# Expert rows of a PEER layer: 32 of 512 gathered rows moved from the preparing steps into the 128 slots

## The chip, the cores and the metric

One core of one Trainium2 chip runs the whole program. The metric is device time in microseconds (us), lower is better, as the median of several runs. TensorE is the matmul engine, VectorE, ScalarE and GpSimd the three others that compute, SyncE issues transfers; the profile calls them PE (PEld for weight loads), DVE, ACT, POOL and SP. Sixteen DMA engines serve the core.

## The reference

Two blocks of a transformer run one behind the other on 512 tokens of width 1024. The change lies in the last large part of the second, the PEER layer: product-key retrieval of experts that are single neurons. For each token, eight heads pick 16 of 16,384 experts each, so 128 experts a token, with softmax weights `g`:

```python
ue = jnp.take(u, ids, axis=0)          # (tokens, heads, 16, 1024)
ve = jnp.take(v, ids, axis=0)
a = jax.nn.gelu(jnp.einsum('cd,chkd->chk', xc, ue), approximate=False)
return jnp.einsum('chk,chkd->cd', (g * a).astype(xc.dtype), ve)
```

## The kernel before, in words

`peer_experts` (L2222) splits the 512 tokens in two halves of 256.

**Sparse half (tokens 0 to 255): gathered rows.** For a tile of 128 tokens (one on each partition) and one of the 128 picks, a *row* is an indirect transfer of 128 x 1024 float32 (512 KB): for each token the table row of its own expert. `row(n)` (L2256) numbers the 512 rows: 128 of `u` and then 128 of `v` for tile 0, and the same for tile 1. A u row is used by one multiply-and-sum on VectorE, the dot product with the token (L2520). After 128 of them ScalarE takes their Gelu (L2447, in `gelu_dots`, which waits until VectorE has used the last one), VectorE multiplies by the softmax weights (L2513), and the 128 v rows are scaled by these and added up (L2524 for the first two, L2527). Rows land in a ring of 8 buffers (`RING`), which lie in the space of xT and hT; GpSimd fetches them (`fetch_rows`, L2332) six rows ahead of their use.

**Dense half (tokens 256 to 511): all experts.** The 128 *slots* (the loop `for s in range(NKEY)` of each engine) stand for 128 experts each. In a slot TensorE multiplies the slot's tile of u (split into a high and a low part by ScalarE L2418 and VectorE L2542, three products each, L110 to L112) with the 256 tokens; ScalarE takes the Gelu (L2463); VectorE multiplies by the slot's gates, which is the slot product L2568; TensorE multiplies with the slot's tile of v into `y_ps` (`down`, L2392). SyncE loads two tiles of 512 KB a slot (`peer_ut` L2297 and `peer_v` L2305), three of each held.

**Gates.** A token's gate for an expert is the softmax weight if it is picked, else 0. They are made in 128 groups of 8 tokens and a quarter of the slots (32) each: one-hots of one half of the expert's number (`one_hot`: on ScalarE as eight squares L2426 and one Relu L2429; in the first 32 groups the even ones on VectorE, L2482), a comparison for the other half (`one_hot_first`, VectorE L2494, one buffer), its product with the weights (`weighed`, GpSimd L2323), eight matmuls on TensorE (`gates`, L2372), and taking the result from PSUM (`take`: ScalarE L2437, VectorE L2504). One-hots, products and PSUM results have two buffers, by the group's parity.

**Order of the work.** Each engine's instructions are issued in one fixed order. The first quarter's 32 groups are made in 32 *preparing steps*, numbered -32 to -1, before slot 0; slot s makes group s + 32 on the side, until slot 95. In the steps before groups 8 and 16 the first two u tiles are split too. `dealt(step)` (L2242) says how many rows VectorE has used by the end of a step or slot: `EARLY` (32) in the preparing steps, one each, and the other 480 over the 128 slots, 3.75 each (three, four, four, four). `use_rows` (VectorE, last thing in each step and slot), `fetch_rows` (GpSimd, `asked` = `dealt` + 6) and `gelu_dots` (ScalarE) all go by it.

```python
    def dealt(step):
        if step < 0:
            return max(0, EARLY * (step + GROUPS + 1) // GROUPS)
        return EARLY + (ROWS - EARLY) * (step + 1) // NKEY
```

By this count tile 0's last u row is used in slot 25 and tile 1's in slot 93, the v rows from slots 26 to 59 and 94 to 127.

Of the kernel before, what the change touches and what calls it, by code (L numbers as in the profile page):

```python
# [2221 lines left out]
def peer_experts(nc, C, xT, hT, h_tok, stream, ids, weights, ut, u, v, u_in, y, x_d):  # L2222
# [10 lines left out]
    GROUPS = DENSE // GROUP  # L2233
    assert GROUPS == QUARTER
    QUARTERS = NKEY // QUARTER
    ROWS = 2 * GT * PICKS
    EARLY = GROUPS
    tok0 = GT * P
    h_dense = hT[:, :, tok0:S]
    rows = [(xT, hT)[r // 4][:, r % 4 * 2:r % 4 * 2 + 2, :].rearrange("p k s -> p (k s)") for r in range(RING)]  # L2240
# [1 line left out]
# [6 lines that stand above are left out]
# [481 lines left out]
def block2(nc, A, C, xT, hT, mod):  # L2729
# [4 lines left out]
    with ExitStack() as ctx:  # L2734
# [48 lines left out]
        with ExitStack() as c2:  # L2783
# [18 lines left out]
            def to_tokens(dve, i, tile):  # L2802
                t, cols, k, toks = at(i)
                return nc.vector.tensor_copy(h_tok[:, t, cols], tile)
            turn(nc, C, GT * KT, lambda i: hT[:, at(i)[2], at(i)[3]], to_tokens)
            peer_experts(nc, C, xT, hT, h_tok, stream, ids, weights, A["peer_ut"], A["peer_u"], A["peer_v"], u_in, yt,
                         dram("x_kept", (P, KT * S)))

# [130 lines left out]
```

## Time and profile before

| | us |
|---|---|
| median of 3 runs | 3567.9 (3562.22 to 3570.99) |
| the profiled execution, its own time | 3575.29 |
| its span | 3573.4 |
| TensorE busy (share of the span) | 3068.4 (86%) |
| VectorE busy | 2337.9 (65%) |
| ScalarE busy | 1389.5 (39%) |
| GpSimd busy | 1101.5 (31%) |
| slot product L2568, first and last start | 2543.8 and 3527.4 |
| DMA, mean over the span | 174 GB/s |

The shares are means over stages that differ; the experts' stage is the last third, from about 2408 us (first transfer of `peer_ut`) to about 3532. In rows of a timeline the first number is the start, the second the duration, and brackets at the end give how long the engine had been idle before and what it waited for. A row `x3` merges three instructions of the same kind. Busy time by stage has for each engine the busy us and the number of instructions, then the granted TensorE clock as a share of its full 2.4 GHz (0.50 is 1.2 GHz), the busy share of the DMA engines and the GB/s that they moved.

### The profile page before, as it was taken

What the parts mean: (1) busy time and instruction counts of PE and PEld (TensorE: products, weight loads), DVE (VectorE), ACT (ScalarE), POOL (GpSimd) and SP (SyncE); (2) the same over time, 40 slices, a digit from 0 to 9 for tenths busy, and PEclk for the clock granted to TensorE, in tenths of its full rate; (3) what the DMA queues carried; (4) which work ended last, traced back from release to release, by engine and by line L of the source; (5) the groups of instructions that cost most, each with busy time, mean ns of one, the idle gap of its engine ahead of it and who ended that gap; (6) DMA issues with size and microseconds to landing.
All of it is one profiled execution on the core that took longest, in us unless ns stands there. A gap on an engine that the chain in (4) does not pass through costs nothing. (4 is left out here: it accounts for less than half of the span.)

```text
span 3573.4 us, 42767 instructions
## 1 busy us (share of the span) xinstructions
PE 3068.4 (86%) x15044; PEld 2316.2 (65%) x15044; DVE 2337.9 (65%) x4087; ACT 1389.5 (39%) x2495; POOL 1101.5 (31%) x781
## 2 busy tenths in 40 slices
PE   7989899998989999995797895634799999999997
PEld 5846688786846678784586663534666776666664
DVE  4256455565347455474645435988998999998886
ACT  3254333212244433312324432115665666665211
POOL 0031000000021100000003101337888888888663
PEclk9969999998959999997898897865799999999998
DMA  5220233353330123351243111106699999999996
GB/s 195 86 80 1 71 94 94 135 182 141 101 91 1 60 88 96 118 194 66 71 137 80 38 48 53 54 20 201 237 377 367 397 406 390 374 377 371 409 409 257
DMA packets 206351, 622.14 MB, mean 174 GB/s; under 512 B 31440, under 2 KB 64624, under 8 KB 200272
## 3 DMA queue, kind: packets, MB, share of 16 engines
q1 hardware_dynamic: 132432, 351.21, 28.5%
q0 software_dynamic: 73728, 268.47, 19.8%
q8 instruction: 110, 1.80, 0.2%
q14 instruction: 81, 0.66, 0.1%
HBM read 598.75 MB, written 20.84 MB: 173 GB/s over the span
## 5 line engine op out<-in xcount | busy, mean ns | idle before, releaser
L110 PE MATMUL psum<-sbuf 128*128 128x512 f32 (+1 forms) x2720 | 1029.0, 378 | 171.1 <-POOL sbuf L2196 84.4
L111 PE MATMUL psum<-sbuf 128*128 128x512 f32 (+1 forms) x2720 | 962.0, 354 | 0.0
L112 PE MATMUL psum<-sbuf 128*128 128x512 f32 (+1 forms) x2720 | 961.2, 353 | 0.0
L110 PEld LDWEIGHTS psum<-sbuf 128*128 128x128 f32 x2720 | 522.8, 192 | 284.3 <-POOL sbuf L2196 86.3
L111 PEld LDWEIGHTS psum<-sbuf 128*128 128x128 f32 x2720 | 523.3, 192 | 106.1 <-issue 36.1
L112 PEld LDWEIGHTS psum<-sbuf 128*128 128x128 f32 x2720 | 521.6, 192 | 72.4
L2392 PE MATMUL psum<-sbuf 128*128 128x512 f32 x1024 | 492.0, 625 | 15.2 <-DVE sbuf L2568 15.2
L1379 POOL TENSOR_TENSOR sbuf<-sbuf 64x768 fp32r<-64x768 f32 (+2 forms) x22 | 29.2, 1328 | 1539.3 <-ACT sbuf L1325 1362.0
L2341 POOL DMA_INDIRECT sbuf<-peer_u,sbuf x256 | 397.4, 1552 | 64.4 <-issue 44.1
L2520 DVE CUSTOM_DVE_ANT_0 sbuf<-sbuf 128x1024 f32<-128x1024 f32 x256 | 379.5, 1510 | 39.7 <-DMA sbuf<-peer_u,sbuf 39.0
L2527 DVE SCALAR_TENSOR_TENSOR sbuf<-sbuf 128x1024 f32<-128x1024 f32 x252 | 339.6, 1385 | 30.9 <-DMA sbuf<-peer_v,sbuf 30.4
L2341 POOL DMA_INDIRECT sbuf<-peer_v,sbuf x256 | 313.6, 1225 | 115.2 <-DVE sbuf L2527 57.0
L2392 PEld LDWEIGHTS psum<-sbuf 128*128 128x128 f32 x1024 | 193.1, 199 | 216.3 <-issue 197.5
L2426 ACT ACTIVATE sbuf<-sbuf 128x128 fp32r<-128x128 f32 x896 | 272.8, 392 | 0.0
L2372 PE MATMUL psum<-sbuf 128*128 128x64 f32 x1024 | 158.8, 308 | 114.0 <-DVE sbuf L2482 52.2
L496 DVE TENSOR_TENSOR sbuf<-sbuf 128x1024 fp32r<-128x1024 f32 x88 | 107.6, 1225 | 207.4 <-ACT sbuf L492 206.9
L2372 PEld LDWEIGHTS psum<-sbuf 128*128 128x128 f32 x1024 | 152.7, 230 | 124.6 <-issue 58.2
L2463 ACT ACTIVATE sbuf<-psum 128x256 f32<-128x256 f32 x128 | 49.1, 384 | 408.3 <-PE psum L112 408.2
L1352 ACT ACTIVATE sbuf<-psum 128x512 f32<-128x512 f32 (+1 forms) x240 | 122.2, 510 | 196.5 <-PE psum L1103 105.3
L2323 POOL TENSOR_TENSOR sbuf<-sbuf 128x512 fp32r<-128x512 f32 x128 | 174.2, 1361 | 48.3 <-DVE sbuf L2494 47.0
L1137 PE MATMUL psum<-sbuf 128*65 128x512 f32 (+4 forms) x384 | 172.2, 537 | 12.0 <-ACT sbuf L1339 11.6
L492 ACT ACTIVATE sbuf<-sbuf 128x1024 fp32r<-128x1024 f32 x88 | 93.1, 1060 | 224.7 <-PE psum L112 224.7
(292 smaller groups left out, 4693.4 us busy)
## 6 DMA issues: line engine op xcount, KB each, us to landing
sbuf<-peer_ut SPq DMA_DIRECT2D x128, 512.0 KB, 8.2
sbuf<-peer_v SPq DMA_DIRECT2D x128, 512.0 KB, 6.7
sbuf<-w_ffn SPq DMA_DIRECT2D x88, 512.0 KB, 3.6
sbuf<-w_mod SPq DMA_DIRECT2D x24, 1024.0 KB, 5.1
sbuf<-w_down SPq DMA_DIRECT2D x16, 1408.0 KB, 6.3
sbuf<-w_fm SPq DMA_DIRECT2D x38, 512.0 KB, 4.6
sbuf<-w_out SPq DMA_DIRECT2D x24, 512.0 KB, 3.7
sbuf<-w_tm SPq DMA_DIRECT2D x10, 1024.0 KB, 5.5
```

The source lines that it names most:

```text
L110: nc.tensor.matmul(acc, w_high(k), x_high(k), start=(k == 0), stop=False)
L111: nc.tensor.matmul(acc, w_high(k), x_low(k), start=False, stop=False)
L112: mm = nc.tensor.matmul(acc, w_low(k), x_high(k), start=False, stop=(k == kt - 1))
L1137: mm = nc.tensor.matmul(summed[0:W, i % SUMS, x.q0[j]:S], v[0:x.kw[j], x.v, j, :], prob[0:x.kw[j], i % 2, j, x.q0[j]:S], start=(j == 0), s ...
L1352: nc.scalar.activation(prob[0:x.kw[j], i % 2, j, x.q0[j]:S], shifted[0:x.kw[j], (block0[i] + j) % 2, x.q0[j]:S], ACT.Exp, scale=HD ** -0.5 ...
L2323: nc.gpsimd.tensor_tensor(part[:, n % 2, :, :, :], equal[:, :, :].unsqueeze(2).to_broadcast([P, GROUP, 2, QUARTER]), halved[:, toks, :].bi ...
L2341: pool.indirect_dma_start(rows[n % RING], None, (u, v)[f], bass.IndirectOffsetOnAxis(ap=stream[:, t, j:j + 1], axis=0)).then_inc(gathered[ ...
L2372: mm = nc.tensor.matmul(g_ps[:, n % 2, 2 * j * QUARTER:2 * (j + 1) * QUARTER], hot[:, n % 2, j, :], part[:, n % 2, j, :, :], start=True, s ...
L2392: mm = nc.tensor.matmul(y_ps[:, 2 * t + half, :], w[:, s % 3, t * P:(t + 1) * P], v_in[:, s % HELD, half * S:(half + 1) * S], start=(s == ...
L2426: nc.scalar.activation(hot[:, n % 2, j, :], C.iota[:, :], ACT.Square, bias=picked[:, 1, at:at + 1], scale=-1.0).then_inc(squared, 1)
L2520: nc.vector.tensor_tensor_reduce(out=rows[r], in0=rows[r], in1=h_tok[:, t, :], scale=1.0, scalar=0.0, op0=ALU.mult, op1=ALU.add, accum_out ...
L2527: nc.vector.scalar_tensor_tensor(sums, rows[r], dots[:, t, j:j + 1], sums, ALU.mult, ALU.add).then_inc(used[r], 1)
```

## The change

`EARLY` goes from 32 to 0. `dealt` is then 0 for all preparing steps and 4 x (s + 1) for slot s, so each slot uses exactly four rows. `asked` is 6 in step -32 (seven before), stays 6 until slot 0, and goes on six ahead of use. The u rows of tile 0 are used in slots 0 to 31, its v rows in 32 to 63, tile 1's in 64 to 95 and 96 to 127. Nothing else changes; the same 512 rows are fetched and used in the same order.

```diff
@@ -2234,7 +2234,7 @@
     assert GROUPS == QUARTER
     QUARTERS = NKEY // QUARTER
     ROWS = 2 * GT * PICKS
-    EARLY = GROUPS
+    EARLY = 0
     tok0 = GT * P
     h_dense = hT[:, :, tok0:S]
     rows = [(xT, hT)[r // 4][:, r % 4 * 2:r % 4 * 2 + 2, :].rearrange("p k s -> p (k s)") for r in range(RING)]
```

## Rows read from the trace of the kernel before

**Rows 1.** The page's 40 slices of 89 us: GB/s moved by DMA.

```profile
GB/s 195 86 80 1 71 94 94 135 182 141 101 91 1 60 88 96 118 194 66 71 137 80 38 48 53 54 20 201 237 377 367 397 406 390 374 377 371 409 409 257
```

**Rows 2.** Busy time by stage: preparing steps, then the slots' four quarters.

```profile
core 0: us, PE busy (x) PEld busy (x) DVE busy (x) ACT busy (x) POOL busy (x), PEclk, DMA share, GB/s
2434.30:2538.10 103.80, 50.86 (x225) 49.01 (x226) 96.98 (x129) 61.34 (x156) 79.72 (x57) 0.50 0.54 162
2543.80:2803.70 259.90, 243.23 (x1276) 174.23 (x1276) 234.95 (x346) 166.39 (x392) 217.49 (x152) 0.95 0.96 361
2803.70:3044.70 241.00, 232.34 (x1278) 169.35 (x1277) 238.78 (x266) 162.93 (x382) 202.27 (x150) 1.00 1.01 398
3044.70:3305.70 261.00, 242.67 (x1274) 173.82 (x1273) 236.30 (x361) 159.97 (x376) 222.59 (x156) 0.96 0.98 375
3305.70:3531.80 226.10, 210.59 (x1007) 141.10 (x1005) 193.95 (x182) 40.24 (x62) 144.32 (x114) 0.98 1.03 409
```

**Rows 3.** Timeline, two preparing steps: start us, us, engine, line, operation.

```profile
2500.64 3.62 PE L2372 MATMUL psum<-sbuf 128*128 128x64 f32 x16 [3.15 <-DVE sbuf L2482]
...
2503.80 2.42 DVE L2520 CUSTOM_DVE_ANT_0 sbuf<-sbuf 128x1024 f32<-128x1024 f32 x1
2504.07 1.05 POOL L2323 TENSOR_TENSOR sbuf<-sbuf 128x512 fp32r<-128x512 f32 x1
2504.30 0.38 ACT L2437 ACTIVATE sbuf<-psum 128x256 f32<-128x256 f32 x1 [1.32 <-PE psum L2372]
...
2506.15 1.21 DVE L2482 TENSOR_TENSOR sbuf<-sbuf 128x1024 fp32r<-128x1024 f32 x1
2507.04 1.15 ACT L2429 ACTIVATE sbuf<-sbuf 128x1024 fp32r<-128x1024 f32 x1
...
2507.41 3.62 PE L2372 MATMUL psum<-sbuf 128*128 128x64 f32 x16 [3.15 <-DVE sbuf L2482]
```

**Rows 4.** Timeline, opening: first fetch, group 2's product, group 3's matmuls.

```profile
2418.79 1.11 POOL L2341 DMA_INDIRECT sbuf<-peer_u,sbuf  x1 [0.17 <-issue]
...
2428.82 1.06 POOL L2323 TENSOR_TENSOR sbuf<-sbuf 128x512 fp32r<-128x512 f32 x1
...
2432.36 1.89 PE L2372 MATMUL psum<-sbuf 128*128 128x64 f32 x8 [0.50 <-issue]
```

**Rows 5.** Timeline around the split of u before group 16.

```profile
2482.56 1.15 ACT L2429 ACTIVATE sbuf<-sbuf 128x1024 fp32r<-128x1024 f32 x1
...
2487.10 3.62 PE L2372 MATMUL psum<-sbuf 128*128 128x64 f32 x16 [7.32 <-DVE sbuf L2482]
```

**Rows 6.** VectorE's waits, last quarter: us in total, times, longest.

```profile
DVE sbuf L2527 <- DMA sbuf<-peer_v,sbuf: 30.4, 46, 1.3
```

**Rows 7.** VectorE's timeline: L2568 of slots 0, 25, 26, 32-34, 60, 93, 94.

```profile
2543.81 0.42 DVE L2568 TENSOR_TENSOR sbuf<-sbuf 128x256 f32<-128x256 f32 x1 [3.37 <-ACT sbuf L2463]
...
2744.76 0.41 DVE L2568 TENSOR_TENSOR sbuf<-sbuf 128x256 f32<-128x256 f32 x1
...
2755.08 0.43 DVE L2568 TENSOR_TENSOR sbuf<-sbuf 128x256 f32<-128x256 f32 x1 [2.38 <-ACT sbuf L2463]
...
2803.66 0.43 DVE L2568 TENSOR_TENSOR sbuf<-sbuf 128x256 f32<-128x256 f32 x1
...
2810.22 0.41 DVE L2568 TENSOR_TENSOR sbuf<-sbuf 128x256 f32<-128x256 f32 x1
...
2817.99 0.41 DVE L2568 TENSOR_TENSOR sbuf<-sbuf 128x256 f32<-128x256 f32 x1
...
3014.21 0.41 DVE L2568 TENSOR_TENSOR sbuf<-sbuf 128x256 f32<-128x256 f32 x1
...
3276.85 0.41 DVE L2568 TENSOR_TENSOR sbuf<-sbuf 128x256 f32<-128x256 f32 x1
...
3288.32 0.42 DVE L2568 TENSOR_TENSOR sbuf<-sbuf 128x256 f32<-128x256 f32 x1 [3.82 <-ACT sbuf L2463]
```

**Rows 8.** Timeline of ScalarE, the Gelu of the second 128 dots.

```profile
3284.19 0.31 ACT L2447 ACTIVATE sbuf<-sbuf 128x128 f32<-128x128 f32 x1 [8.21 <-DVE sbuf L2520]
```

## The prediction

> **What bounds the kernel now.** I read the page's slices first: the change touches only the experts' stage, the last third of the span, where DMA rises from some 200 GB/s to a plateau of 367 to 409 [rows 1]. Then busy time by stage [rows 2]. The 32 preparing steps (2434 to 2538 us) keep VectorE at 97 of 104 us while the transfers move 162 GB/s and TensorE is half idle. In the 128 slots everything is near full at once: DMA share 0.96 to 1.03, TensorE 93 to 96%, VectorE 86 to 99%. So the present kernel uses 32 rows in a stretch with idle DMA and puts 3.75 a slot, not 4, where DMA is full. The change gives that up.
>
> Last I read the order of time. A pair of steps [rows 3] takes 6.77 us (TensorE's 16 gate matmuls begin at 2500.64 and again at 2507.41), and VectorE is what it waits for: its one-hot of the even group (L2482) comes only at 2506.15, behind two row dots. A dot is drawn out to 2.4 us because it stands beside GpSimd's 1.05 us product (rows 3: 2503.80 and 2504.07).
>
> **The preparing steps without rows.** Without the dots, next in line is a loop between ScalarE and TensorE over the odd groups, whose one-hots share one buffer: ScalarE takes the gates at 2504.30, makes eight squares and ends its Relu at 2507.04 + 1.15 = 2508.19, so 3.89 us; then 8 gate matmuls, half of the 3.62 us, 1.81; two handoffs of about 0.07. That is 5.85 us a pair. VectorE's own remaining work (1.21 + 4 x 0.41) and GpSimd's two products (2 x 1.05) fit beside it. Between group 3 and group 31 are 14 pairs.
> - Now: from 2432.36 + 1.89 = 2434.25 [rows 4] to the end of the stretch [rows 2], 2538.1, so 103.9 us. 14 x 6.77 is 94.8; the other 9.1 are the two splits of u (before groups 8 and 16), where VectorE waits for ScalarE's split, splits, and only then makes the even one-hot: from the Relu's end (2482.56 + 1.15 = 2483.71) to the end of both groups (2487.10 + 3.62 = 2490.72) 7.0 us [rows 5].
> - After: 14 x 5.85 = 81.9, plus 2 x (7.1 - 1.9) = 10.4, since a normal pair then ends 1.9 after its Relu. Together 92.3: a gain of 11.6 us.
> - Opening: GpSimd's product for group 2 starts at 2428.82, behind seven row fetches begun at 2418.79 [rows 4]. Afterwards there are six, at about 1.25 apart, so it starts near 2426.3; with VectorE free, group 3 ends near 2431.1 and not 2434.25: 3.2 us.
> Sum: **-14.8 us**. Bounds: 0 (the steps bound elsewhere) and -19 (both splits hidden as well). ScalarE's way from group 31 to the first slot product stays the same length, and just moves forward. No instruction is dropped: the 32 row fetches and dots go to the slots.
>
> **The slots with four rows.** A slot loads 2 tiles of 512 KB and its rows of 512 KB (0.524 MB) each: 3.015 MB now, 3.146 after. At the 409 GB/s of the last quarter [rows 2] that is 7.37 and 7.69 us.
> - Last quarter: it is DMA's; VectorE there waited 30.4 us for v rows [rows 6]. 8 rows x 1.28 us = **+10.3**.
> - Second quarter (v rows, gates being made): VectorE is 99% busy and DMA at 398 GB/s. Slots of three and four rows take 6.56 and 7.77 (2803.66, 2810.22, 2817.99 in rows 7), and three of four slots have four. With four everywhere: 32 x 7.77 = 248.6 against 241: **+7.6**. TensorE, busy 232 / 32 = 7.3 us a slot there, stays just under.
> - First and third quarter (u rows): 25 slots in 200.95 us (2543.81 to 2744.76) and 33 in 262.6 (3014.21 to 3276.85), 8.04 and 7.96 a slot [rows 7], well above both the 7.37 of the bytes and the 7.47 that the second quarter's mix of slots needs ((3 x 7.77 + 6.56) / 4). Such a slot with four rows is not shown by itself. Lower bound 7.77 (as with v rows), upper 8.7 (the first quarter's 361 GB/s). I take 8.33: the 8.0 plus a quarter row at 1.21 (rows 7, 7.77 - 6.56) to 1.28 (DMA), which is also the same transfer rate held (3.015/8.0 = 377 GB/s; 3.146/377 = 8.34). 64 slots: 533.1.
> - The two handovers from u to v rows: ScalarE stops until the last dot (8.21 us [rows 8]), then makes a one-hot before its Gelu, and VectorE idles 3.82; a slot of 10.3 and one of 11.5 come of it [rows 7], each followed by a long one, about 5 to 6 us too much in all. The first moves from slot 25 to 31 and stays, 5.9. The second moves from slot 93 to 95, after which no one-hot is left: 1. So 533.1 + 6.9 = 540.0 for both quarters, against 259.9 + 261.0 = 520.9: **+19.1**.
>
> Slots: 10.3 + 7.6 + 19.1 = **+37.0 us**. All of it lies on the path, since no other work stands behind the slots: the stage ends with the last rows and the last slot.
>
> The DMA ceiling is the term to weigh. The rows show 409 GB/s at a share of 1.03. The Trainium skill (DMA: Bandwidth & Descriptors, Where 436 GB/s comes from) puts the ceiling of the 16 engines at 435 GB/s. By that a four-row slot would be 7.23 us and the last quarter 15 us shorter, the whole change about +7. The trace never shows such a rate, so I stay with 409.
>
> **Sum.** -14.8 + 37.0 = +22.2 us. The profiled execution took 3575.3 (span 3573.4), so it would take 3597.5; it lies 7.4 above the median of 3567.9, and the median would be 3567.9 + 22.2 = **3590 us**. A measurement of this kernel can tell about 0.3% (10.7 us) from no change.
>
> **Rivals.**
> - A, as forecast: 0.60. Its own range 3580 to 3601, u slots of 8.17 to 8.5.
> - B, faster: the even deal makes the u slots regular. They are jittery now (waits for rows, clock 0.95), and their rows come in 4, 4, 4, 3. If four-row u slots run like four-row v slots, 64 x (8.33 - 7.77) = 36 us go, so 22.2 - 35.8 = -13.6: 3554. It decides below 7.82 us a u slot ((22.2 + 10.7) / 64 is 0.51). For it: DMA moves only 361 and 375 GB/s there. Against: the share is 0.96 to 0.98 even so, which is 5% more engine time per byte than in the last quarter, and an even deal doesn't make a packet quicker. The Trainium skill (SBUF — State Buffer, SBUF: two separate sides) says that an engine's work cannot slow a transfer; by that the low rate would be thin demand and could rise to 409. The rows of the u quarters rather speak against it. 0.07.
> - C, no change: the jitter gives back part of that. Between 7.82 and 8.15 us a u slot the total is within 10.7 us; at the present 8.0 it is 22.2 - 64 x 0.33 = +1: 3569. 0.13.
> - D, slower still: TensorE's clock. In the second quarter TensorE is 96% busy and the granted clock 1.00; in the u quarters it is 93% busy and the clock 0.95 and 0.96 [rows 2]. Four rows leave it idle longer in every slot. If the second quarter falls to the level of the others, its slots go from 7.77 to 8.33: 32 x 0.56 = +18, 3608. 0.13.
> - E: the preparing steps gain nothing, because the chain from VectorE's comparison (L2494) over GpSimd's product (L2323) and back, one buffer long, is as slow as the dots were: 3605. Against it: 0.41 + 1.05 us and two handoffs are half of a step's 2.9. 0.07.
> - That the rows aren't moved can be excluded: the deal is 0 for every step below 0. Six rows are still fetched ahead, as now.
>
> **How the numbers follow.** Predicted time: A, 3590. The range 3570 to 3610 leaves out B and the lower half of C (0.07 + 0.07) and some 0.05 above D. Slower than 0.3%: A + D + E = 0.80; same 0.13; faster 0.07.
>
> **What the profile should show.** Pairs of steps of 5.8 to 5.9 us with TensorE's gates released by ScalarE's Relu (L2429), no longer by L2482; group 31 done near 2523, first L2568 near 2529; DMA nearly idle from 2435 to there. Slots of 7.77 in the second quarter without a short one; 7.69 in the last, at 409 GB/s; first to last L2568 near 1021 us (983.6 now, rows 7). Pairs still at 6.8, or u slots at 8.0 or less, would prove me wrong.

## The result and the profile after

The changed kernel takes **3609.0 us** (median of 4, 3601.74 to 3619.13) against 3569.07 (median of 4) for the kernel before in the same series: a ratio of 1.0116, interval 1.0094 to 1.0138. Slower by 40 us where 22 were forecast; the sign was right, the size nearly twice. The profiled execution took 3619.13 (span 3617.3, against 3573.4), 10 above its median.

The first view is the page of the changed kernel, GB/s by slice of 90 us, the counterpart of [rows 1]:

```profile
GB/s 191 88 77 1 71 93 94 143 169 143 99 87 1 68 90 99 131 183 44 90 156 38 37 71 41 41 82 24 328 373 373 379 403 396 366 376 362 409 409 254
```

The 201 and 237 GB/s at the end of the preparing steps have become 24 and the start of the plateau. The plateau still has its two levels: 362 to 376 in slices where u rows are dotted, 396 to 409 where v rows are added (379 is the slice behind 2803 us, with most of the first handover).

Busy time by stage of the changed kernel (us, then busy us of PE, PEld, DVE, ACT, POOL with instructions, granted clock, DMA share, GB/s), which answers to [rows 2]:

```profile
2434.00:2531.00 97.00, 56.54 (x242) 53.57 (x243) 42.94 (x76) 60.54 (x158) 31.89 (x31) 0.50 0.10 36
...
2536.45:2808.30 271.85, 243.00 (x1266) 173.15 (x1264) 246.09 (x385) 164.68 (x386) 236.21 (x160) 0.95 0.97 364
2808.30:3063.70 255.40, 245.59 (x1314) 176.68 (x1314) 250.11 (x259) 170.11 (x395) 207.61 (x161) 0.99 1.01 396
3063.70:3335.40 271.70, 246.54 (x1252) 174.01 (x1251) 243.95 (x383) 156.90 (x366) 234.67 (x158) 0.94 0.98 365
3335.40:3571.00 235.60, 207.86 (x998) 139.57 (x996) 199.09 (x186) 40.23 (x61) 157.86 (x124) 0.99 1.03 409
```

In the preparing steps VectorE is now busy 43 of 97 us and no longer the bound. Their pairs, in the timeline of the changed kernel (start, us, engine, line), as in [rows 3]:

```profile
2504.06 1.15 ACT L2429 ACTIVATE sbuf<-sbuf 128x1024 fp32r<-128x1024 f32 x1
...
2505.26 3.78 PE L2372 MATMUL psum<-sbuf 128*128 128x64 f32 x16 [2.12 <-ACT sbuf L2429]
...
2505.85 1.22 DVE L2482 TENSOR_TENSOR sbuf<-sbuf 128x1024 fp32r<-128x1024 f32 x1
...
2509.96 1.15 ACT L2429 ACTIVATE sbuf<-sbuf 128x1024 fp32r<-128x1024 f32 x1
...
2511.16 3.78 PE L2372 MATMUL psum<-sbuf 128*128 128x64 f32 x16 [2.12 <-ACT sbuf L2429]
```

From 2505.26 to 2511.16 is 5.90 us, released by ScalarE's Relu: 5.85 was forecast, with that releaser.

**Where the time went.** I divide the stage at fixed events: its first load of a u tile, and the first L2568 of slots 0, 32, 64, 96 and 127. All are us of one profiled execution; the rows below the second are the experiments.

| kernel | preparing | slots 0-31 (u) | 32-63 (v) | 64-95 (u) | 96-127 (v) | all slots |
|---|---|---|---|---|---|---|
| before | 135.5 | 259.8 | 241.0 | 261.0 | 221.7 | 983.5 |
| changed | 121.7 | 271.8 | 255.4 | 271.8 | 235.6 | 1034.6 |
| changed, again | 121.7 | 275.8 | 254.9 | 268.4 | 235.8 | 1034.9 |
| 16 rows early | 122.4 | 265.3 | 245.5 | 270.2 | 226.0 | 1007.0 |
| changed, no v tiles loaded | 121.7 | 278.6 | 253.9 | 275.8 | 199.9 | 1008.2 |
| before, no v tiles loaded | 134.5 | 249.8 | 242.2 | 263.7 | 195.3 | 951.1 |
| changed, product only | 121.1 | 253.2 | 254.9 | 248.2 | 234.2 | 990.5 |
| changed, light dot | 121.7 | 254.9 | 255.0 | 248.6 | 233.3 | 991.9 |
| changed, half product | 121.2 | 257.8 | 254.2 | 255.8 | 235.2 | 1003.0 |
| changed, late Gelu | 121.1 | 275.8 | 250.7 | 270.0 | 235.2 | 1031.7 |
| before, light dot | 135.6 | 248.7 | 240.5 | 245.1 | 222.1 | 956.5 |
| before, light dot, late Gelu | 134.6 | 240.7 | 239.4 | 237.7 | 225.2 | 943.0 |
| changed, v table | 121.7 | 273.7 | 255.5 | 269.6 | 234.6 | 1033.3 |

Of the 43.9 us between the two spans, 6.5 lie ahead of the stage, where the code is the same (its first u load is at 2408.3 before and 2414.8 after). The preparing steps give 13.8, the slots cost 51.1, and the rest is 0.1. So the stage itself loses 37.3.

**The queue that the forecast left out.** These are GpSimd's groups in the changed kernel, first in slots 0 to 31, then in 32 to 63 (line, form, count | busy us, mean ns | idle before them and what ended it). L2341 fetches a row, L2323 is the one-hot's product:

```profile
L2341 POOL DMA_INDIRECT sbuf<-peer_u,sbuf x122 | 191.1, 1566 | 32.5 <-issue 22.6 <-DVE sbuf L2494 8.5
L2323 POOL TENSOR_TENSOR sbuf<-sbuf 128x512 fp32r<-128x512 f32 x32 | 37.2, 1164 | 10.0 <-DVE sbuf L2494 9.4
...
L2341 POOL DMA_INDIRECT sbuf<-peer_v,sbuf x123 | 143.0, 1163 | 32.7 <-issue 30.1
L2323 POOL TENSOR_TENSOR sbuf<-sbuf 128x512 fp32r<-128x512 f32 x32 | 58.7, 1835 | 12.9 <-DVE sbuf L2494 12.9
```

And one u slot of GpSimd's timeline in the changed kernel:

```profile
2700.24 1.07 POOL L2323 TENSOR_TENSOR sbuf<-sbuf 128x512 fp32r<-128x512 f32 x1
2701.47 1.78 POOL L2341 DMA_INDIRECT sbuf<-peer_u,sbuf  x1 [0.16 <-issue]
2703.55 0.94 POOL L2341 DMA_INDIRECT sbuf<-peer_u,sbuf  x1 [0.30 <-issue]
2704.79 1.71 POOL L2341 DMA_INDIRECT sbuf<-peer_u,sbuf  x1 [0.30 <-DVE sbuf L2494]
2706.81 1.98 POOL L2341 DMA_INDIRECT sbuf<-peer_u,sbuf  x1 [0.31 <-issue]
2708.81 1.22 POOL L2323 TENSOR_TENSOR sbuf<-sbuf 128x512 fp32r<-128x512 f32 x1
```

The slot takes 8.57 us (2700.24 to 2708.81), and nothing in it is idle but 0.3 us ahead of each fetch, in which the engine issues. A fetch takes 0.94 us or nearly twice that. With the mean of the group a u slot costs GpSimd 4 x 1.56 + 3 x 0.30 + 0.16 + 1.16 = 8.46 us; slots 0 to 31 took 8.49 in the mean. In the slots with v rows the same engine, at the same four fetches, has a mean fetch of 1.16, waits 12.9 us ahead of its products for VectorE's comparison (L2494), and the median slot is 7.78. Busy shares hide this: 236.21 of 271.85 us is 87%, but with the issue gaps, 0.30 us ahead of 96 fetches and 0.16 ahead of 32, it is 270.1, or 99%. In the row above, 9.4 of the 10.0 us idle ahead of L2323 lie before the first product, where the window begins; between a fetch and the next product all gaps of the quarter together are 0.5 us. An engine that never waits for another's signal is not paced by TensorE, whose clock was 0.95 here, or by the transfers.

The kernel before had it all in its trace. GpSimd's groups in its slots 0 to 31:

```profile
L2341 POOL DMA_INDIRECT sbuf<-peer_u,sbuf x90 | 140.1, 1557 | 23.8 <-issue 15.6 <-DVE sbuf L2494 6.1
L2323 POOL TENSOR_TENSOR sbuf<-sbuf 128x512 fp32r<-128x512 f32 x32 | 41.5, 1298 | 13.6 <-DVE sbuf L2494 13.2
```

The fetch of a u row took 1.56 us there too. With 3.75 of them a slot, 2.75 x 0.30 + 0.16 of gaps and a product of 1.22 us (the mean of slots 0 to 24; the 1.30 of the row counts the longer ones of the last slots too), a slot is 5.84 + 0.98 + 1.22 = 8.04 us, and [rows 7] gave 8.04. That it agrees so well is in part chance: GpSimd waited another 6.8 us in these 25 slots, and 92 fetches fell into them, not 94. A quarter of a row more is 0.25 x 1.86, which makes 8.50: the slot that came. This sum I had not made.

### The profile page after: what moved, and what is told of

It is laid out like the page before. It is cut to its first block and busy times, and to the rows that moved or that the text cites. A ratio compares the mean times of both kernels' runs of the same rounds, so it can differ in the third digit from the quotient of the medians.

```text
span 3617.3 us, 42767 instructions
## 1 busy us (share of the span) xinstructions
PE 3096.0 (86%) x15044; PEld 2331.0 (64%) x15044; DVE 2315.5 (64%) x4087; ACT 1391.4 (38%) x2495; POOL 1094.7 (30%) x781
## 5 line engine op out<-in xcount | busy, mean ns | idle before, releaser
L2392 PE MATMUL psum<-sbuf 128*128 128x512 f32 x1024 | 501.9, 636 | 28.2 <-DVE sbuf L2568 28.2
L2341 POOL DMA_INDIRECT sbuf<-peer_u,sbuf x256 | 393.8, 1538 | 68.3 <-issue 48.1
L2520 DVE CUSTOM_DVE_ANT_0 sbuf<-sbuf 128x1024 f32<-128x1024 f32 x256 | 354.5, 1412 | 45.6 <-DMA sbuf<-peer_u,sbuf 44.0
L2527 DVE SCALAR_TENSOR_TENSOR sbuf<-sbuf 128x1024 f32<-128x1024 f32 x252 | 339.2, 1380 | 37.2 <-DMA sbuf<-peer_v,sbuf 37.0
L2341 POOL DMA_INDIRECT sbuf<-peer_v,sbuf x256 | 314.8, 1230 | 110.7 <-DVE sbuf L2527 55.0
L2323 POOL TENSOR_TENSOR sbuf<-sbuf 128x512 fp32r<-128x512 f32 x128 | 169.8, 1326 | 93.1 <-DVE sbuf L2494 92.1
```

What stands on the lines that cost most here:

```text
L2323: nc.gpsimd.tensor_tensor(part[:, n % 2, :, :, :], equal[:, :, :].unsqueeze(2).to_broadcast([P, GROUP, 2, QUARTER]), halved[:, toks, :].bi ...
L2341: pool.indirect_dma_start(rows[n % RING], None, (u, v)[f], bass.IndirectOffsetOnAxis(ap=stream[:, t, j:j + 1], axis=0)).then_inc(gathered[ ...
L2392: mm = nc.tensor.matmul(y_ps[:, 2 * t + half, :], w[:, s % 3, t * P:(t + 1) * P], v_in[:, s % HELD, half * S:(half + 1) * S], start=(s == ...
L2520: nc.vector.tensor_tensor_reduce(out=rows[r], in0=rows[r], in1=h_tok[:, t, :], scale=1.0, scalar=0.0, op0=ALU.mult, op1=ALU.add, accum_out ...
L2527: nc.vector.scalar_tensor_tensor(sums, rows[r], dots[:, t, j:j + 1], sums, ALU.mult, ALU.add).then_inc(used[r], 1)
```

## The experiments

The theories, by letter: **D**, the u slots go at the speed of the transfers, as my sum assumed. **V**, at the speed of VectorE's dots. **G**, at the speed of GpSimd's queue, whose fetches are drawn out beside the dots. **L**, a loop of ScalarE and TensorE sets the pair of preparing steps as soon as VectorE has no more than one row in it. The expectations of the runs without v tiles still use V for what is divided here into V and G.

**The changed kernel again**, unchanged, as the base of the first series.

> The changed kernel as it is, beside the others of this job. In its first profile the preparing steps gained 13.9 us and the 127 slot intervals cost 51.2 us, while 6.5 us of the 44 lay in stages before the experts. Theory S (slots cost more than forecast, the rest is scatter): median 37 to 41 us above the kernel before; in the profile again about 122 us from the first u tile's load to the first slot product, and about 1030 to 1035 us from the first to the last slot product. Rival N (most of the excess over the forecast of 22 us is scatter of one profile): median 20 to 30 us above, slot intervals near 1021 us.

3605.4 us (before 3570.24; ratio 1.0104, interval 1.0079 to 1.013), so 35.2 above, a little less than the 37 to 41 expected. The stage repeats within 0.3 us (121.7 and 1034.9), though single quarters differ by 4. So less than 4 us in one quarter proves nothing.

**Half of the rows early.**

```
-    EARLY = 0
+    EARLY = GROUPS // 2
```

> EARLY = 16: one row in every second preparing step, 496 over the slots (3.875 each). Theory L (a loop of ScalarE and TensorE bounds the pair of preparing steps at 5.9 us as soon as VectorE has no more than one row in it): pairs of 5.9 to 6.1 us, so the preparing steps keep nearly all of the 14 us gain, and the slots cost half of 51 us: +12 us on the kernel before, 3580. Rival P (rows cost the preparing steps in proportion): half of both, +19 us, 3588.

3584.57 us, ratio 1.0043 (1.0027 to 1.0059). The median is 14.3 above its kernel before, where 12 were expected. The preparing steps keep nearly all they gained (122.4, so 13.1 of 13.8), and the slots pay 23.5 of the 51.1. Sixteen of the 32 early rows, one in every second step, therefore cost 0.7 us where they stood; the other 16 cost 13.1 there.

**No v tiles loaded**, once on the changed kernel and once on the kernel before: the first tiles are used again and 2.6 MB instead of 3.1 MB are moved in a slot.

```
-                if s >= HELD:
-                    sp.wait_ge(y_made, s - HELD + 1)
-                sp.dma_start(v_in[:, s % HELD, :], v[s * P:(s + 1) * P, :]).then_inc(v_landed[s % HELD], 16)
+                if s < HELD:
+                    sp.dma_start(v_in[:, s % HELD, :], v[s * P:(s + 1) * P, :]).then_inc(v_landed[s % HELD], 16)
...
-                pe.wait_ge(v_landed[s % HELD], 16 * (s // HELD + 1))
+                pe.wait_ge(v_landed[s % HELD], 16)
```

> EARLY = 0, and the dense half's v tiles are loaded for the first three slots only and used again after that: 125 transfers of 512 KB less, the dense half's down products are made from the wrong tiles. A slot then moves 2.62 MB in place of 3.15, 6.4 us at 409 GB/s. Theory D (transfers bind the u slots and the last quarter): last quarter from 7.6 to about 6.5 us a slot (TensorE), u slots from 8.45 to 7.6 to 7.8, second quarter stays at 7.8 to 7.9 (VectorE); in all some 80 us less than the changed kernel, 3530. Rival V (VectorE and GpSimd get in each other's way over u rows, transfers are only slow because they are asked for late): u slots stay at 8.3 to 8.5, only the last quarter falls, 35 us less, 3574.

> The same with EARLY = 32: v tiles loaded for the first three slots only. Read against the EARLY = 0 kernel without v tiles. Theory D: the last quarter then costs the same with 3.75 and with 4 rows (TensorE's 6.5 us), u and v slots of the other quarters differ by VectorE's quarter row, 0.3 us each, 29 us in all, less the 14 us of the preparing steps: the EARLY = 0 kernel is 12 to 16 us slower. Rival V: the price of the rows is VectorE's and stays, EARLY = 0 is 30 to 40 us slower.

3577.72 us (ratio 1.002, 1.0006 to 1.0034) and 3541.53 us (0.993, 0.9906 to 0.9954): 36.2 us apart, as with all tiles loaded (35.2 in this series). Busy time by quarter and one wait of VectorE (total, times, longest) in the changed kernel without v tiles:

```profile
2530.70:2809.20 278.50, 245.87 (x1265) 175.15 (x1264) 236.05 (x384) 164.55 (x386) 242.70 (x160) 0.94 0.87 297
...
3063.20:3339.00 275.80, 247.06 (x1251) 173.49 (x1250) 233.38 (x384) 156.90 (x366) 240.62 (x157) 0.94 0.88 300
3339.00:3538.90 199.90, 199.01 (x999) 137.47 (x997) 195.84 (x187) 40.19 (x61) 149.52 (x125) 1.00 1.02 403
```

```profile
DVE sbuf L2519 <- DMA sbuf<-peer_u,sbuf: 36.2, 23, 3.7
```

The last quarter, which is DMA's, falls from 235.6 to 199.9. The u quarters do not fall at all, at 297 and 300 GB/s, and VectorE still waits for rows, up to 3.7 us at a time. With a sixth of the bytes gone and the rows still late, what they are late for is not the transfers: **D falls**. The row is asked for late. (In the kernel before, the first u quarter did get 10.0 us shorter without v tiles, and the third 2.7 longer; whether that is scatter is not shown.)

**The dot in another form of instruction.** First only the product, without the sum along the row:

```
-                    nc.vector.tensor_tensor_reduce(out=rows[r], in0=rows[r], in1=h_tok[:, t, :], scale=1.0,
-                                                   scalar=0.0, op0=ALU.mult, op1=ALU.add,
-                                                   accum_out=dots[:, t, j:j + 1]).then_inc(used[r], 1)
+                    nc.vector.scalar_tensor_tensor(rows[r], rows[r], C.ones[:, 0:1], h_tok[:, t, :],
+                                                   ALU.mult, ALU.mult).then_inc(used[r], 1)
```

> EARLY = 0, with the dot's multiply-and-sum (L2520) replaced by VectorE's three-operand product that v rows use (L2527), same tiles, no sum: the dots stay a constant, so the sparse half's sums are of wrong weights. Theory G (in u slots GpSimd sets the pace: four fetches of 1.56 us and gaps of 0.3 us, one product of 1.17, no idle time besides; the fetch is drawn out from 0.94 to 1.8 us by the form of VectorE's dot): fetches fall to the 1.16 us of v slots, u slots from 8.4 to 7.8 us, both u quarters together 35 to 45 us shorter: about 3565. Rival F (a fetch from the u table is slow by itself, or TensorE's clock makes the long slots): fetches stay at 1.5 us, u slots at 8.4 us, no change against the changed kernel, 3605.

3564.31 us, ratio 1.0002 (0.9988 to 1.0015): the whole loss against the kernel before with its old dot is gone with one line. Then the same instruction with the sum (`accum_out=dots[:, t, j:j + 1]`), so that the dot is complete:

> EARLY = 0, and the dot is made by the three-operand product with its sum written out (two instructions again, the second reads the accumulator); everything is computed. Theory G1 (the form of the multiply makes the fetches slow): u slots near 7.8 us, 3565 to 3575. Theory G2 (the second instruction, which reads the accumulator between two products, gives GpSimd its bad moments): u slots stay at 8.4, 3605, while the kernel without the sum is at 7.8.

3565.04 us, ratio 0.9995 (0.9983 to 1.0007). I call this form the light dot. Its kernel by stage, GpSimd's groups in slots 0 to 31, and GpSimd's timeline of one u slot:

```profile
2527.50:2782.40 254.90, 235.42 (x1265) 169.85 (x1264) 250.01 (x384) 165.41 (x386) 206.58 (x160) 0.98 1.00 393
...
3037.40:3286.00 248.60, 237.08 (x1269) 170.06 (x1268) 248.26 (x383) 157.86 (x366) 206.12 (x160) 0.99 1.02 402
```

```profile
L2341 POOL DMA_INDIRECT sbuf<-peer_u,sbuf x122 | 141.1, 1156 | 32.4 <-issue 30.5
L2323 POOL TENSOR_TENSOR sbuf<-sbuf 128x512 fp32r<-128x512 f32 x32 | 59.0, 1845 | 19.5 <-DVE sbuf L2494 19.5
```

```profile
2701.53 1.90 POOL L2323 TENSOR_TENSOR sbuf<-sbuf 128x512 fp32r<-128x512 f32 x1 [0.23 <-DVE sbuf L2494]
2703.57 1.78 POOL L2341 DMA_INDIRECT sbuf<-peer_u,sbuf  x1 [0.15 <-issue]
2705.66 0.93 POOL L2341 DMA_INDIRECT sbuf<-peer_u,sbuf  x1 [0.30 <-issue]
2706.90 0.94 POOL L2341 DMA_INDIRECT sbuf<-peer_u,sbuf  x1 [0.30 <-issue]
2708.14 0.94 POOL L2341 DMA_INDIRECT sbuf<-peer_u,sbuf  x1 [0.30 <-issue]
2709.31 1.90 POOL L2323 TENSOR_TENSOR sbuf<-sbuf 128x512 fp32r<-128x512 f32 x1 [0.23 <-DVE sbuf L2494]
```

A dot and the fetch that begins 0.05 us behind it, first in the changed kernel, then with the light dot:

```profile
2706.76 1.21 DVE L2520 CUSTOM_DVE_ANT_0 sbuf<-sbuf 128x1024 f32<-128x1024 f32 x1
2706.81 1.98 POOL L2341 DMA_INDIRECT sbuf<-peer_u,sbuf  x1 [0.31 <-issue]
...
2706.85 1.30 DVE L2520 SCALAR_TENSOR_TENSOR sbuf<-sbuf 128x1024 f32<-128x1024 f32 x1
2706.90 0.94 POOL L2341 DMA_INDIRECT sbuf<-peer_u,sbuf  x1 [0.30 <-issue]
```

What a drawn-out fetch waits for can be read from the traces. In slots 0 to 31 of the changed kernel 89 of 128 fetches take over 1.3 us; each began inside a VectorE operation (57 in a dot, 32 in the split L2542) and ended 0.81 to 0.85 us after that operation's end. With the light dot there are 32 such of 128, and they end 0.84 to 0.85 us after. So a fetch waits for the row-wide VectorE operation that it finds running, in either form. The forms differ where a fetch begins 0.05 to 0.1 us behind the dot (slots 0 to 30 and 64 to 94): beside the old form all 27 took 1.94 to 1.98 us, beside the light one all 46 took 0.93 to 0.94. In the two slots shown light dots begin 1.21 us apart and short fetches 1.24, so fetch after fetch can fall on the start of a dot; the old dots begin 1.15 apart. That this keeping in step is why three of four stay short is a reading of the traces; no run tests it apart from the form.

VectorE's work has not become less: 250.01 busy us in slots 0 to 31 against 246.09, in a stretch 17 us shorter. So **V falls**: the dots' own time does not set the pace of the changed kernel. What became shorter is GpSimd's fetch, 1.57 to 1.16 us in the mean, three of four now at 0.94. GpSimd then waits for VectorE's comparison (L2494) before its product, u slots run at 7.79 almost without jitter, and VectorE is 98 to 100% busy. The transfers went from 364 and 365 GB/s to 393 and 402 with not a byte changed.

That the low rate had been thin demand is what the Trainium skill (SBUF — State Buffer, SBUF: two separate sides) would have had me read: a transfer is not slowed by an engine's work, but descriptors (the orders for the DMA engines) that GpSimd has to write can come late, which it tells of VectorE's 2-port modes. The two rates above agree. The page counts a VectorE operation with two SBUF inputs as one that contends with GpSimd's SBUF reads, and the second to come as blocked until the first is done. The products that begin inside the split (1.90 us, ending 0.91 us after it) agree with that, and the fetches behave alike. The page makes no difference between two operations with two inputs; both forms of the dot have two, and the traces show 1.57 against 1.16 us a fetch, and 1.94 to 1.98 against 0.94 at the same start. On that difference the measurement decides.

**Half of GpSimd's product**, with VectorE's work and the dots as in the changed kernel: a separate way to shorten GpSimd's queue.

```
-                nc.gpsimd.tensor_tensor(part[:, n % 2, :, :, :],
+                x = 2 if n < 2 else 1
+                nc.gpsimd.tensor_tensor(part[:, n % 2, :, 0:x, :],
```

> EARLY = 0, and GpSimd's product of every group from 2 on is made for the high part of the weights only (256 columns, not 512); the low part is that of groups 0 and 1, so gates are off by rounding. Theory G: GpSimd's product takes 0.6 in place of 1.05 us and every u slot with gates gets shorter by about 0.4 us: 64 x 0.4 = 26 us, 3580; the second quarter, where VectorE is full, gains less. Rival D (transfers) or C (TensorE's clock): no change in the u slots, 3605.

3575.67 us, ratio 1.0028 (1.0014 to 1.0041). GpSimd's groups in slots 0 to 31:

```profile
L2342 POOL DMA_INDIRECT sbuf<-peer_u,sbuf x122 | 181.8, 1490 | 32.4 <-issue 21.8 <-DVE sbuf L2495 8.5
L2324 POOL TENSOR_TENSOR sbuf<-sbuf 128x256 fp32r<-128x256 f32 x32 | 31.4, 982 | 11.0 <-DVE sbuf L2495 10.5
```

The two groups hold 15.1 us less than in the changed kernel (191.1 + 37.2 - 181.8 - 31.4), and the quarter is 14.0 shorter (271.8 to 257.8). The quarter with v rows, where GpSimd had time to spare, moves by 1.2. That is G, shown a second time without touching the dot. The product fell by 0.18 us in the mean, not by the 0.45 expected, and each fetch by 0.08 as well; the median is 11.1 above its kernel before, 24 less than the 35.2 of the changed kernel, for the 26 forecast. The granted clock rose from 0.95 to 0.98 in this quarter with the dot as it was, so here the clock came with the shorter slots.

**The Gelu of the dots one slot later**, since that handover was a term of my sum: ScalarE's `gelu_dots` stands ahead of the slot's own Gelu and take, for the dots of the slot before.

```
                 if s + 2 < NKEY:
                     split_u(s + 2)
+                gelu_dots(s - 1)
                 if s + GROUPS < QUARTERS * GROUPS:
                     take(s + GROUPS)
-                gelu_dots(s)
```

> EARLY = 0, and ScalarE takes the Gelu of the 128 dots in the slot after their last one, behind that slot's one-hot, Gelu and split, so that it doesn't stop for VectorE's last dots. Theory H (this stop makes slots 31 and 32 of 11.5 and 10.9 us, some 6 us too much; at slot 95 it costs nothing since no one-hot is left): slots 31 and 32 near 8.3 and 7.9 us, the others unchanged, 6 us less than the changed kernel, 3599. Rival: these two slots are long because of the switch from u to v rows in GpSimd's fetches and stay.

3599.36 us, ratio 1.0088 (1.0057 to 1.012). First, from the changed kernel's timeline, the L2568 of slots 31, 32 and 33 and ScalarE's Gelu of the first 128 dots (2804.14, behind a wait of 8.27 us), then VectorE's slots 31 to 33 in this kernel:

```profile
2796.81 0.41 DVE L2568 TENSOR_TENSOR sbuf<-sbuf 128x256 f32<-128x256 f32 x1
...
2804.14 0.31 ACT L2447 ACTIVATE sbuf<-sbuf 128x128 f32<-128x128 f32 x1 [8.27 <-DVE sbuf L2520]
...
2808.27 0.42 DVE L2568 TENSOR_TENSOR sbuf<-sbuf 128x256 f32<-128x256 f32 x1 [3.82 <-ACT sbuf L2463]
...
2819.12 0.43 DVE L2568 TENSOR_TENSOR sbuf<-sbuf 128x256 f32<-128x256 f32 x1 [3.44 <-ACT sbuf L2463]
```

```profile
2788.11 0.41 DVE L2567 TENSOR_TENSOR sbuf<-sbuf 128x256 f32<-128x256 f32 x1
...
2797.22 0.42 DVE L2567 TENSOR_TENSOR sbuf<-sbuf 128x256 f32<-128x256 f32 x1
...
2805.26 0.41 DVE L2567 TENSOR_TENSOR sbuf<-sbuf 128x256 f32<-128x256 f32 x1
```

Slots 31 and 32 take 9.11 and 8.04 instead of 11.46 and 10.85: 5.2 us less, where I had priced the handover at 5.9. All slots together are only 2.9 shorter, and the interval overlaps that of the changed kernel repeated, so in the time of the kernel no gain is shown: beside the slow fetches, other u slots scatter by more than this.

**The light dot in the kernel before.** Same edit of the dot, rows still early.

> EARLY = 32 (the kernel before) with the dot made by the three-operand product and its sum; everything is computed. With the kernel of EARLY = 0 and this dot (3565, slots 991.9 us) it shows what the change costs when fetches are not drawn out. Theory G: u slots at the 7.47 us of (3 x 7.78 + 6.54) / 4, so 64 x 0.53 = 34 us less than the kernel before, slots near 950, 3531; the change would then cost 992 - 950 - 14 = 28 us in place of 37. Rival: the form of the dot also sets the pace of the preparing steps, where a dot stands drawn out to 2.0 and 2.4 us; if pairs of steps fall from 6.77 to 5.9 us, 10 us more go, 3521, and the change costs nearly 40 us.

3544.03 us against 3568.42, ratio 0.9942 (0.9921 to 0.9962): 24 us less, where 37 were expected; the slots came to 956.5 and not to 950. The preparing steps stay as they were (135.6), as the timeline of two of them shows:

```profile
2501.74 3.62 PE L2372 MATMUL psum<-sbuf 128*128 128x64 f32 x16 [3.15 <-DVE sbuf L2482]
...
2504.90 2.41 DVE L2520 SCALAR_TENSOR_TENSOR sbuf<-sbuf 128x1024 f32<-128x1024 f32 x1
...
2508.51 3.62 PE L2372 MATMUL psum<-sbuf 128*128 128x64 f32 x16 [3.15 <-DVE sbuf L2482]
```

The pair is 6.77 us as in [rows 3], and a dot beside GpSimd's product takes 2.41: there it is VectorE that is drawn out, in either form. The slots fall from 983.5 to 956.5, nearly all in the u quarters (11.1 and 15.9). This gives the change **without** the slow fetches: from this kernel to the changed one with the light dot, preparing steps -13.9, slots +35.4, together +21.5 us. The medians, each against its own series' kernel before (+0.5 and -24.4), give +24.8.

**The kernel before with the light dot and the late Gelu**, with the v row that shared slot 25 with the last u rows dealt one slot later (`return n - 1 if n in (PICKS + 1, 3 * PICKS + 1) else n`; the second value, 385, does not occur, since slot 93 ends at 384). So no v row waits in the slot of the last dot for a Gelu that now comes a slot later.

> EARLY = 32, the dot by the three-operand product with its sum, ScalarE's Gelu of the dots one slot late, and slot 25 stops at row 127, so that no v row waits inside it; everything is computed. Expected: the gain of the new dot, and of each of the two handovers (10.3 and 10.3, 11.5 and 10.0 us now) 5 us back: 8 to 10 us below the kernel with the new dot alone, 3522, faster than both kernels. Rival: only the first slot of each handover gets shorter, 4 us.

**3526.5 us** (3522.94 to 3537.51), ratio 0.9893 (0.9871 to 0.9915): the fastest of all, 42 us below the kernel before and 77 to 82 below the change, each against its own series. Its u quarters by stage:

```profile
2535.00:2775.70 240.70, 234.69 (x1280) 170.67 (x1280) 238.19 (x346) 167.63 (x395) 201.08 (x151) 0.99 0.99 390
...
3015.10:3252.80 237.70, 231.80 (x1268) 168.31 (x1267) 237.54 (x360) 157.37 (x366) 198.03 (x153) 1.00 1.02 403
```

Against the light dot alone they are 8.0 and 7.4 us shorter, more than the 5 us forecast for each handover, and the medians are 17.5 us apart, not 8 to 10. Slots 25 and 26 together fall by 6.2 us, 93 and 94 by 6.9. Why it is more than priced is open. The last quarter gives back 3.1.

**Another table.** To exclude that the u rows' place in memory makes their fetch slow, all rows are fetched from v:

```
-                    pool.indirect_dma_start(rows[n % RING], None, (u, v)[f],
+                    pool.indirect_dma_start(rows[n % RING], None, v,
```

> EARLY = 0, and u rows are gathered from the v table as well; the dots are those of wrong rows. Theory G: no change, fetches of 1.56 us and u slots of 8.4 us, 3600 to 3605, since the instruction and not the table matters. Rival T (where the u table lies in memory makes its packets slow): u slots near 7.8 us, 3565.

3604.39 us, ratio 1.0104 (1.0083 to 1.0124). GpSimd's fetches in slots 0 to 31:

```profile
L2341 POOL DMA_INDIRECT sbuf<-peer_v,sbuf x128 | 197.4, 1542 | 34.2 <-issue 25.7 <-DVE sbuf L2494 7.9
```

1.54 us a fetch from v, beside dots, as from u (1.57), and 1.16 from v beside the additions of v rows. It is the neighbour on VectorE that matters, not the table.

## What the prediction had right, and the step that failed

The rise was forecast with the right sign and at little more than half its size: 22.2 us for 39.9. That 3609.0 still lies inside 3570 to 3610, by 1.0 us, is no support: the upper end was drawn there for another mechanism, TensorE's clock, which did not come.

- **Preparing steps, -14.8: right.** Measured -13.8 (13.9 with the light dot). Pair 5.90 for 5.85, with the releaser named; the transfers there fell to 36 GB/s. Rival E did not come. (The sum takes 7.1 us for a split where its row gives 7.0, some 0.2 us in all.)
- **Last quarter, +10.3: 3.7 too little.** Measured 13.9 at the same 409 GB/s, which is 5.7 MB more and not the 4.2 of 8 rows. In 235.6 us at 409 GB/s 184 transfers of 524 kB pass, in 221.7 us 173: nearly 3 more than the deal adds. The kernel before comes into the quarter with more fetched ahead: at the first L2568 of slot 96 GpSimd had issued 399 fetches there and 389 in the changed kernel, ten apart where the deal has eight; the rest of the nearly three was under way. I priced the rows of the quarter and not the stock at its edge.
- **Second quarter, 7.77 a slot: right, and short in the sum.** The median slot is 7.78, but slots 33 to 63 average 7.89, since slot 33, slots 39 to 42 and the one that ends a tile of tokens (slot 63, 9.27) are longer: 3.7 us over 31 slots that I had taken all at the best value.
- **Handovers: right to 1 us.** Slots 31 and 32 together 22.3 for my 22.0, slot 95 7.80 for 9.33.
- **The u slots: the failed step.** It is the sentence "which is also the same transfer rate held", with its 8.33. Slots 0 to 30 took 8.40 and 64 to 94 took 8.52, so the number missed by only 7.8 us over 62 slots, but its ground was wrong: taking a sixth of the bytes away left the slots as long, and another form of the dot brought them to 7.79, nearly my lower bound. The pace is that of GpSimd's queue, its fetches lengthened by the VectorE operations that they wait for. The trace of before had it: an added u row costs 1.56 + 0.30 = 1.86 us of GpSimd's time, and I priced it at 1.21 to 1.28. That the number came within 2% of the slot was luck.
- **Rival B had the mechanism and not the outcome.** I set thin demand against a DMA share of 0.96 and called the rows rather against it. They were not: share 0.87 at 297 GB/s goes with slots just as long, and 393 to 402 GB/s came when the fetches did. But an even deal does not thicken the demand, it lengthens the queue that thins it; so B's 3554 could not come with the old dot. With the light dot in both kernels the change is still slower, by some 21 to 25 us, because the u slots of the kernel before gain as well.
- **Rival D did not come.** The granted clock was 0.99 in the second quarter and its slots 7.78. There was one dip there, and the u quarters stand at 0.95 and 0.94 as before (0.95 and 0.96).

By terms, the slots' miss of 14 us is u slots 7.8, v slots of the second quarter 3.7, last quarter 3.7, handovers -1.2; the preparing steps add 1.0. The stage then is 37.3 slower and not 22.2. The medians differ by 39.9, whose interval (33.5 to 49.3) holds that.

The two 22s must not be confused: the forecast +22.2 agrees with the +21.5 between the two kernels with the light dot, since there a slot goes by VectorE and by the bytes, as my sum had it in effect. It is not evidence for the reason I gave for the kernel as it was.

Open is why a fetch 0.05 to 0.1 us behind the start of one form of the dot is held up and behind the other isn't, with both reading two rows of 1024 and nearly equal durations, and how much of the gain comes from that and how much from the two engines keeping in step. Nor was the longer run of slots 39 to 42 traced to a cause.

## What to carry to other kernels

Before an engine with a modest busy share is ruled out as the pace, add what it spends on issuing: here GpSimd read 87% and was at 99%. A DMA share near 1 and a low rate do not prove that transfers are the bound; take bytes away and see whether the stretch gets shorter. And when rows are moved between stages, count each queue that issues something for them, at the duration that the issue has beside its neighbours in the new place.

## What was unexpected of the hardware

- A fetch of 128 rows holds GpSimd for 0.94 us, or for up to 1.99 us when it begins inside a longer VectorE operation, and it then ends 0.81 to 0.85 us after that one's end (89 of 128 fetches in slots 0 to 31 of the changed kernel). The mean is 1.57 us beside dots made with `tensor_tensor_reduce` and 1.16 us beside the same dots made with `scalar_tensor_tensor` and `accum_out`. VectorE's own time hardly differs. On the changed kernel that is 3605.4 us (+35.2 to its kernel before) against 3565.04 (+0.5).
- GpSimd's product is 1.16 us with the first form and 1.85 with the second, but not for the form of the dot. With the light dot GpSimd waits for L2494 and its product begins 0.22 us into the split (L2541 there), ending 0.91 us after it: 1.90 us in 29 of 31 slots, as in most of slots 32 to 63 of the changed kernel. In the changed kernel GpSimd is late and 30 of 31 products fall beside dots, at 1.05 to 1.35 us. As there are four fetches and one product in a slot, four short fetches outweigh the longer product.
- The granted clock followed: 0.95 and 0.94 in the u quarters with the first form, 0.98 and 0.99 with the second, where TensorE is busy 92 and 95% of the stretch against 89 and 91%.
